# Moving the split operand tile to the end of on-chip memory in a one-core, two-block fp32 network

## The chip, the cores and the metric

The kernel runs on one core of a Trainium2 chip. That core has four engines which compute: TensorE (PE in the profile, with its weight loads as a row of their own, PEld), VectorE (DVE), ScalarE (ACT) and GpSimd (POOL). SyncE (SP) issues most of the DMAs. All of them run at the same time and meet at semaphores. The metric is the device time of one execution in microseconds, the median of several runs.

## What is computed

Input and output are one sequence of 256 tokens of width 1024 in float32. Two networks of two layers each follow one another.

```
def first_block(x, ...):                       # DEPTH = 2
    for i in range(DEPTH):
        if i % 2 == 0:
            mix = attention_mixer(x, ...)      # 8 windowed query heads over 2 key heads, 8 neighbourhood heads
        else:
            mix = mamba2_bidir_mixer(x, ...)   # 32 heads, both directions
        x = layer_norm(DN_ALPHA * x + mix, ...)
        x = layer_norm(DN_ALPHA * x + squared_relu_mlp(x, mlp_w1[i], mlp_w2[i]), ...)   # width 4096
...
def swiglu(h, w_gate, w_up, w_down):           # second block, twice in each of 2 layers, width 2816
    return (jax.nn.silu(h @ w_gate) * (h @ w_up)) @ w_down
```

The second block's layers are: half a swiglu, a mixer with a causal convolution on one half of the channels and differential attention on the other, and another swiglu, with an RMS norm ahead of each. Nearly all arithmetic is in products of the 256 tokens with weight matrices, all float32.

## The kernel before

**Work.** Weights come from HBM in units of 1 MB, that is 2048 floats in each of 128 partitions. A product is done at float32 accuracy with operands of the type float32r: weights and activations are each split into a high part (a cast) and a low part (the value less its high part), and three products are added in PSUM: high by high, low weight by high activation, high weight by low activation.

**The rings.** `w_raw`, `w_hi` and `w_lo` are rings of three units. SP loads a unit to `w_raw` (L626 and its like), ACT casts it to `w_hi` (L842), DVE (L1363), or POOL in some stages (L742), subtracts to `w_lo`, PE multiplies. Each step waits on semaphores for the one ahead, and for the slot of the ring to be free.

**The split operand.** `op` is the activations' counterpart: 16 chunks, each with a high half and a low half of 256 floats in every partition (`op_hi`, `op_lo`), 32 KB in each partition. ACT writes high halves (L857, L942 and some more), DVE low halves (L1401, L1509 and some more). No DMA touches it. PE reads it in two ways:

- as the moving operand, streamed past resident weights: `project_pair` (L2144 to L2148), where one matmul takes a whole chunk, high and low joined, as 512 columns against `w_hi`, and one takes the high half's 256 columns against `w_lo`; and `feature_chunk` (through L2070), where each of the three terms streams 256 columns of `op`;
- as the stationary operand, 128 columns loaded to the array, with 512 columns of `w_hi` or `w_lo` moving (`output`, `output_part` and `wide_tile`, through L2070).

**The loops.** `mlp` and `swiglu` are loops over groups of units: project one or two units to PSUM, let ACT and DVE form the hidden activations (into chunks 8 to 11 of `op`), multiply these by a unit of the second matrix into `acc`. The order of each engine's instructions is written out in the program, and nothing in it depends on where tiles lie.

**Placement.** Tiles are allocated one behind another in the order of the `sb(...)` lines. Each start is rounded up to a multiple of 32 bytes, and the first lies at byte 16,512 of the partition. Bytes within a partition:

| tile | before | after |
|---|---|---|
| `w_raw`, `w_hi`, `w_lo` | 16,512 to 90,240 | the same |
| `op` | 90,240 to 123,008 | 196,320 to 229,088 |
| `X` up to `g_pair`, 23 tiles | 123,008 to 165,600 | 90,240 to 132,832 |
| `arena` | 165,600 to 229,088 | 132,832 to 196,320 |

`arena` is carved by hand into each stage's own tiles. In the attention stage it starts with 2304 floats of constants, then `q_raw` 1024, `r_tmp` 1024, `k_raw` 256, `QT` 2048 and `KT`, six chunks of 256 floats. Heads 8 and 9 of the 16 read chunk 2 of `KT` at L2362, heads 12 and 13 chunk 4.

Of the kernel before, what the change touches and what calls it, by code (L numbers as in the profile page):

```python
# [9 lines left out]
F32R = mybir.dt.float32r  # L10
# [4 lines left out]
P = 128  # L15
T = 256
# [179 lines left out]
def two_blocks(nc, A, out):  # L196
    with ExitStack() as ctx:
        def sb(name, shape, dt=F32):
            return ctx.enter_context(nc.sbuf_tensor(name, shape, dt))
# [5 lines left out]
        w_raw = sb("w_raw", [P, RING, UN])  # L205
        w_hi = sb("w_hi", [P, RING, UN], F32R)
        w_lo = sb("w_lo", [P, RING, UN], F32R)
        op = sb("op", [P, 16, 2, T], F32R)
        op_hi, op_lo = op[:, :, 0, :], op[:, :, 1, :]
        X = sb("X", [P, TT, D])  # L210
        xn = sb("xn", [P, TT, D])
        turn_buf = sb("turn_buf", [P, 2, 2, T])
# [19 lines left out]
        g_pair = sb("g_pair", [P, TT, 2, P], F32R)  # L232
        AR = 15872
        arena = sb("arena", [P, AR])

        acc = ctx.enter_context(nc.psum_tensor("acc", [P, 4, 512], F32))
        pg = ctx.enter_context(nc.psum_tensor("pg", [P, 4, 512], F32))
# [2597 lines left out]
```

## Time and profile before

| | us |
|---|---|
| runs (3) | 1749.53, 1749.56, 1749.89 |
| median | 1749.56 |
| profiled execution: its span | 1748.3 |
| TensorE busy in that span | 1724.1 (99%) |
| VectorE busy | 1178.8 (67%) |
| ScalarE busy | 924.4 (53%) |
| GpSimd busy | 283.0 (16%) |

The page gives for the profiled execution its span alone, from the first to the last instruction; the median of the runs is 1.3 us above it. "Busy" of TensorE counts overlapping, pipelined matmuls, so 99% doesn't mean that its array is full: the distance between the starts of two matmuls says how fast it goes.

### The profile page before, as it was taken

The page shows a single profiled execution, that of the slowest core. Times are in us where ns is not written, and L with a number is a line of the kernel's source. Part 1 is how long each engine was busy: PE and PEld are TensorE (multiplying, and loading weights), DVE is VectorE, ACT ScalarE, POOL GpSimd, SP SyncE. Part 2 cuts the span into 40 slices and gives each one's busy share as a digit, 9 for nine tenths or more (in the row PEclk, how much of TensorE's full clock was granted, in tenths as well). Part 3 has the DMA queues.
Part 4 walks back from the last instruction along what each step waited for, and adds up shares of the span by engine and source line. Part 5 has one row for each costly group of instructions (what it writes and reads, how often), then busy time and mean ns, then how long its engine had stood idle before and what let it go on. Part 6 is the DMA issues. An engine that isn't in the chain of part 4 may idle for free.

```text
span 1748.3 us, 25220 instructions
## 1 busy us (share of the span) xinstructions
PE 1724.1 (99%) x9721; PEld 1472.5 (84%) x9721; DVE 1178.8 (67%) x1573; ACT 924.4 (53%) x1269; POOL 283.0 (16%) x154
## 2 busy tenths in 40 slices
PE   8999999999999999999999999999999999999999
PEld 7767888899798788878888978888888889878887
DVE  5767766778666776576666785666666667956665
ACT  4455444544675544455445666544554456665443
POOL 3000300376261040010000640000000006500000
PEclk9999999999999999999999999999999999999999
DMA  9314655564603575546555432655465555426652
GB/s 303 115 54 163 217 190 187 155 182 141 240 1 103 166 236 193 182 142 195 190 191 188 164 131 96 210 189 185 161 208 187 189 185 169 145 85 204 192 190 98
DMA packets 204268, 293.90 MB, mean 168 GB/s; under 512 B 6474, under 2 KB 169776, under 8 KB 204192
## 3 DMA queue, kind: packets, MB, share of 16 engines
q1 hardware_dynamic: 201072, 285.62, 50.3%
q0 software_dynamic: 2688, 6.47, 1.4%
q8 instruction: 52, 0.85, 0.2%
q10 hardware_dynamic: 432, 0.75, 0.1%
q14 instruction: 24, 0.20, 0.0%
HBM read 291.77 MB, written 1.05 MB: 167 GB/s over the span
## 4 chain that ended last, share of the span: by engine, by line
PE 92%; DVE 4%; ACT 3%; POOL 1%; issue 1%; DMA 0%; SPq 0%; ACTq 0%; DVEq 0%; POOLq 0%
PE acc L2070 30%; PE pg L2070 15%; PE pg L2144 12%; PE pg L2148 12%; PE pg L2147 6%; PE pg L2145 6%; PE acc L2575 1%; PE pg L2362 1%; PE pg L2562 1%; PE pg L2677 1%; PE pg L2190 1%; POOL w_lo L742 1%; ACT op L857 1%; DVE op L1401 1%; PE pg L2391 0%
## 5 line engine op out<-in xcount | busy, mean ns | idle before, releaser
L1363 DVE TENSOR_TENSOR w_lo<-w_raw,w_hi 128x2048 fp32r<-128x2048 f32 x231 | 538.9, 2334 | 162.9 <-ACT w_hi L842 162.8
L842 ACT CAST w_hi<-w_raw 128x2048 fp32r<-128x2048 f32 x269 | 513.0, 1908 | 70.8 <-PE pg L2070 28.3
L2070 PE MATMUL acc<-w_hi,op 128*128 128x512 f32 x1600 | 518.3, 393 | 1.7 <-DVE op L2000 1.6
L2144 PE MATMUL pg<-op,w_hi 128*128 128x512 f32 x960 | 382.3, 398 | 7.0 <-DVE op L1393 1.9
L2148 PE MATMUL pg<-op,w_hi 128*128 128x512 f32 x960 | 379.7, 396 | 0.0
L2070 PEld LDWEIGHTS acc<-w_hi,op 128*128 128x128 f32 x1600 | 300.4, 188 | 67.5 <-issue 8.6
L2070 PE MATMUL acc<-w_lo,op 128*128 128x512 f32 x800 | 311.5, 389 | 0.0
L742 POOL TENSOR_TENSOR w_lo<-w_raw,w_hi 128x2048 fp32r<-128x2048 f32 x38 | 175.1, 4615 | 682.6 <-DVE w_lo L1363 630.3
L2147 PE MATMUL pg<-op,w_lo 128*128 128x256 f32 x960 | 267.6, 279 | 0.0
L2145 PE MATMUL pg<-op,w_lo 128*128 128x256 f32 x960 | 266.3, 277 | 0.0
L2070 PE MATMUL pg<-op,w_hi 128*128 128x256 f32 x1184 | 222.6, 286 | 2.8 <-DVE op L1401 1.2
L2147 PEld LDWEIGHTS pg<-op,w_lo 128*128 128x128 f32 x960 | 180.2, 188 | 44.3 <-DVE op L1387 0.9
L2145 PEld LDWEIGHTS pg<-op,w_lo 128*128 128x128 f32 x960 | 180.5, 188 | 39.7
L2144 PEld LDWEIGHTS pg<-op,w_hi 128*128 128x128 f32 x960 | 182.1, 190 | 16.9 <-issue 4.8
L2070 PEld LDWEIGHTS pg<-op,w_hi 128*128 128x128 f32 x1184 | 187.3, 192 | 6.6 <-issue 3.1
L2148 PEld LDWEIGHTS pg<-op,w_hi 128*128 128x128 f32 x960 | 179.9, 187 | 0.0
L2070 PEld LDWEIGHTS acc<-w_lo,op 128*128 128x128 f32 x800 | 150.4, 188 | 30.0
L2070 PE MATMUL pg<-op,w_lo 128*128 128x256 f32 x592 | 167.6, 283 | 0.0
L942 ACT CAST op<-h 128x512 fp32r<-128x512 f32 x76 | 47.2, 621 | 215.1 <-PE acc L2070 189.8
L1509 DVE TENSOR_TENSOR op<-h,op 128x512 fp32r<-128x512 f32 x76 | 57.0, 750 | 84.9 <-ACT op L942 84.9
L2070 PEld LDWEIGHTS pg<-op,w_lo 128*128 128x128 f32 x592 | 113.7, 192 | 0.6 <-issue 0.5
L924 ACT COPY act_buf<-pg 128x512 f32<-128x512 f32 x44 | 25.8, 586 | 115.1 <-PE pg L2148 115.0
(348 smaller groups left out, 1735.5 us busy)
## 6 DMA issues: line engine op xcount, KB each, us to landing
w_raw<-in_mlp_w SPq DMA_DIRECT2D x64, 1024.0 KB, 5.3
w_raw<-in_ffn_w_gate SPq DMA_DIRECT2D x44, 1024.0 KB, 5.3
w_raw<-in_ffn_w_up SPq DMA_DIRECT2D x44, 1024.0 KB, 5.3
w_raw<-in_ffn_w_down SPq DMA_DIRECT2D x44, 1024.0 KB, 4.8
w_raw<-in_ssm_w_in SPq DMA_DIRECT2D x24, 1024.0 KB, 5.4
w_raw<-in_w_in SPq DMA_DIRECT2D x20, 1024.0 KB, 5.0
w_raw<-in_attn_w_in SPq DMA_DIRECT2D x8, 1024.0 KB, 10.6
w_raw<-in_ssm_w_out SPq DMA_DIRECT2D x8, 1024.0 KB, 4.9
```

Source lines behind the costliest of these rows:

```text
L742: pool.tensor_tensor(w_lo[:, r, :], w_raw[:, r, :], w_hi[:, r, :].bitcast(F32), ALU.subtract) \
L842: act.copy(w_hi[:, u % RING, :], w_raw[:, u % RING, :]).then_inc(hi_ready, 1)
L857: ins = act.activation(op_hi[:, j, :] if bias is None else turn_buf[:, b % 2, c, :], turn_out(name, b)[:, c * T:(c + 1) * T], ACT.Identity ...
L924: act.copy(act_pair, low_half(0)).then_inc(gate_lo, 1)
L942: act.copy(op_hi[:, at_chunk:at_chunk + 2, :], h32[:, :].rearrange("p (c t) -> p c t", c=2)).then_inc(h_hi, 1)
L1363: dve.tensor_tensor(w_lo[:, s, :], w_raw[:, s, :], w_hi[:, s, :].bitcast(F32), ALU.subtract) \
L1509: dve.tensor_tensor(op_lo[:, dst, :], h32[:, :].rearrange("p (c t) -> p c t", c=2), op_hi[:, dst, :].bitcast(F32), ALU.subtract).then_inc( ...
L2070: ins = pe.matmul(psum, l, r, start=first and i == 0, stop=last and i == 2)
L2144: pe.matmul(bank, hi, joined, start=k == 0, stop=False)
L2145: pe.matmul(bank[:, 0:T], lo, op_hi[:, k, :], start=False, stop=False)
L2147: pe.matmul(bank[:, 0:T], lo, op_hi[:, k, :], start=False, stop=False)
L2148: ins = pe.matmul(bank, hi, joined, start=False, stop=k == KC - 1)
```

## The change

The allocation of `op` moves from behind `w_lo` to behind `arena`. The tile's shape, its views and every instruction stay. Two kinds of addresses change: `op` starts 106,080 bytes further on, and everything that lay behind it (`X` to `arena`) starts 32,768 bytes earlier. The first step is an odd multiple of 32, the second a multiple of 128. The number and the order of the instructions on each engine are the same in both programs.

```
         w_lo = sb("w_lo", [P, RING, UN], F32R)
-        op = sb("op", [P, 16, 2, T], F32R)
-        op_hi, op_lo = op[:, :, 0, :], op[:, :, 1, :]
         X = sb("X", [P, TT, D])
...
         AR = 15872
         arena = sb("arena", [P, AR])
+        op = sb("op", [P, 16, 2, T], F32R)
+        op_hi, op_lo = op[:, :, 0, :], op[:, :, 1, :]
```

## Rows read from the trace of the kernel before

**Rows 1.** The page: span, busy time by engine, granted clock by slice
```profile
span 1748.3 us, 25220 instructions
...
PE 1724.1 (99%) x9721; PEld 1472.5 (84%) x9721; DVE 1178.8 (67%) x1573; ACT 924.4 (53%) x1269; POOL 283.0 (16%) x154
...
PEclk9999999999999999999999999999999999999999
```

**Rows 2.** The page: the chain that ended last, by engine
```profile
PE 92%; DVE 4%; ACT 3%; POOL 1%; issue 1%; DMA 0%; SPq 0%; ACTq 0%; DVEq 0%; POOLq 0%
```

**Rows 3.** The page: groups by line; out<-in (moving first), count | busy, mean ns | idle before
```profile
L2070 PE MATMUL acc<-w_hi,op 128*128 128x512 f32 x1600 | 518.3, 393 | 1.7 <-DVE op L2000 1.6
L2144 PE MATMUL pg<-op,w_hi 128*128 128x512 f32 x960 | 382.3, 398 | 7.0 <-DVE op L1393 1.9
L2148 PE MATMUL pg<-op,w_hi 128*128 128x512 f32 x960 | 379.7, 396 | 0.0
...
L2070 PE MATMUL acc<-w_lo,op 128*128 128x512 f32 x800 | 311.5, 389 | 0.0
...
L2147 PE MATMUL pg<-op,w_lo 128*128 128x256 f32 x960 | 267.6, 279 | 0.0
L2145 PE MATMUL pg<-op,w_lo 128*128 128x256 f32 x960 | 266.3, 277 | 0.0
L2070 PE MATMUL pg<-op,w_hi 128*128 128x256 f32 x1184 | 222.6, 286 | 2.8 <-DVE op L1401 1.2
...
L2070 PE MATMUL pg<-op,w_lo 128*128 128x256 f32 x592 | 167.6, 283 | 0.0
```

**Rows 4.** PE in order of time, swiglu loop, one cycle of four chunks: start, us
```profile
896.70 0.39 PE L2144 MATMUL pg<-op,w_hi 128*128 128x512 f32 x1
896.93 0.28 PE L2145 MATMUL pg<-op,w_lo 128*128 128x256 f32 x1
897.04 0.28 PE L2147 MATMUL pg<-op,w_lo 128*128 128x256 f32 x1
897.16 0.40 PE L2148 MATMUL pg<-op,w_hi 128*128 128x512 f32 x1
897.39 0.40 PE L2144 MATMUL pg<-op,w_hi 128*128 128x512 f32 x1
897.63 0.28 PE L2145 MATMUL pg<-op,w_lo 128*128 128x256 f32 x1
897.75 0.27 PE L2147 MATMUL pg<-op,w_lo 128*128 128x256 f32 x1
897.86 0.40 PE L2148 MATMUL pg<-op,w_hi 128*128 128x512 f32 x1
898.09 0.39 PE L2144 MATMUL pg<-op,w_hi 128*128 128x512 f32 x1
```

**Rows 5.** The same view just behind: `op` stationary, the rings moving
```profile
900.88 0.39 PE L2070 MATMUL acc<-w_hi,op 128*128 128x512 f32 x1
901.11 0.39 PE L2070 MATMUL acc<-w_lo,op 128*128 128x512 f32 x1
901.34 0.62 PE L2070 MATMUL acc<-w_hi,op 128*128 128x512 f32 x2
901.79 0.39 PE L2070 MATMUL acc<-w_lo,op 128*128 128x512 f32 x1
```

**Rows 6.** DVE in order of time in the same stretch, three successive slots
```profile
896.85 0.69 DVE L1496 TENSOR_TENSOR act_buf<-act_buf,xn 128x512 f32<-128x512 f32 x1
897.93 2.29 DVE L1363 TENSOR_TENSOR w_lo<-w_raw,w_hi 128x2048 fp32r<-128x2048 f32 x1 [0.39 <-ACT w_hi L842]
...
903.58 2.29 DVE L1363 TENSOR_TENSOR w_lo<-w_raw,w_hi 128x2048 fp32r<-128x2048 f32 x1 [0.33 <-ACT w_hi L842]
...
908.99 2.29 DVE L1363 TENSOR_TENSOR w_lo<-w_raw,w_hi 128x2048 fp32r<-128x2048 f32 x1 [1.12 <-ACT w_hi L842]
```

**Rows 7.** PE in order of time, state-space stage: operands from `g_pair` and `neg_tri`
```profile
475.76 0.34 PE L2562 MATMUL pg<-g_pair,select 128*128 128x384 f32 x1
475.94 0.28 PE L2564 MATMUL pg<-neg_tri,ident_r 128*128 128x256 f32 x1
476.05 0.34 PE L2562 MATMUL pg<-g_pair,select 128*128 128x384 f32 x1
```

**Rows 8.** PE in order of time: scores of heads 8, 9, 12 and 13
```profile
93.89 1.13 PE L2362 MATMUL pg<-arena 64*128 64x256 f32 x4
...
96.55 1.13 PE L2362 MATMUL pg<-arena 64*128 64x256 f32 x4
...
103.31 1.13 PE L2362 MATMUL pg<-arena 64*128 64x256 f32 x4
...
107.55 1.13 PE L2362 MATMUL pg<-arena 64*128 64x256 f32 x4
```

**Rows 9.** DVE by form, 512 floats; last, one line's min/median/max ns
```profile
L1509 DVE TENSOR_TENSOR op<-h,op 128x512 fp32r<-128x512 f32 x76 | 57.0, 750 | 84.9 <-ACT op L942 84.9
...
L1501 DVE TENSOR_TENSOR h<-pg,h 128x512 f32<-128x512 f32 x44 | 30.4, 691 | 55.5 <-ACT h L935 55.5
...
L1792 DVE TENSOR_TENSOR arena<-arena,acc 128x512 f32<-128x512 f32 x32 | 22.0, 687 | 24.0 <-POOL arena L789 23.7
...
L1393 DVE TENSOR_TENSOR op<-turn_buf,op 128x512 fp32r<-128x512 f32 x12 | 8.3, 692 | 0.4
...
L1509 DVE TENSOR_TENSOR op<-h,op x76: 687/692/2883, 156.9 to 1737.0; 128x512 fp32r<-128x512 f32 x76
```

**Rows 10.** ACT's groups by form, 512 floats in every partition
```profile
L942 ACT CAST op<-h 128x512 fp32r<-128x512 f32 x76 | 47.2, 621 | 215.1 <-PE acc L2070 189.8
...
L929 ACT ACTIVATE act_buf<-act_buf 128x512 f32<-128x512 f32 x44 | 27.7, 629 | 6.8 <-DVE act_buf L1496 6.8
...
L1007 ACT ACTIVATE arena<-arena 128x512 f32<-128x512 f32 x4 | 2.5, 632 | 1.1 <-DVE arena L1923 1.1
```

More of the change, by code:

```diff
@@ L207, in two_blocks @@
         w_lo = sb("w_lo", [P, RING, UN], F32R)
-        op = sb("op", [P, 16, 2, T], F32R)
-        op_hi, op_lo = op[:, :, 0, :], op[:, :, 1, :]
         X = sb("X", [P, TT, D])
@@ L234, in two_blocks @@
         arena = sb("arena", [P, AR])
+        op = sb("op", [P, 16, 2, T], F32R)
+        op_hi, op_lo = op[:, :, 0, :], op[:, :, 1, :]
         acc = ctx.enter_context(nc.psum_tensor("acc", [P, 4, 512], F32))
```

## The prediction

> **What bounds the kernel now.** I read the page from the top. The granted clock is full in every slice, so TensorE runs at its upper level, 2.4 GHz, throughout, and PE is busy for 1724.1 of 1748.3 us [rows 1]. The chain that ended last is PE for 92% of the span [rows 2]. The largest groups are all matmuls with `op` on one side and a weight ring on the other, and the idle time ahead of them is a few us in all [rows 3]. So the kernel is bound by the rate at which PE gets through its list, and it hardly ever waits for somebody. A change of addresses can move the end only if it changes how fast one matmul follows another, or if it makes writers of `op` so slow that PE has to wait for them.
>
> How fast is that rate? Rows of the time order give the distances between starts. Where 512 columns move, the next matmul starts 0.23 us later: three matmuls from 900.88 to 901.34 are 0.46 us for two, and five from 900.88 to 901.79 are 0.91 us for four, 227 to 228 ns each [rows 5]. At 2.4 GHz 512 columns are 213 ns, so about 14 ns lie between them. Where `op` moves, four chunks (four matmuls of 512 and four of 256 columns) take 898.09 - 896.70 = 1.39 us [rows 4]; 3072 columns are 1280 ns, so eight matmuls leave about 110 ns, again 14 ns each.
>
> **The change part by part.** It removes, adds and moves no instruction, no wait and no DMA. What it can alter is one of four things.
>
> (1) *The distance between `op` and the rings.* PE reads both at once. If neighbours in memory got in each other's way, the distance between starts would depend on which chunk meets which slot. In the trace it doesn't: L2144 to L2148 run through chunks 0 to 7, which start 24.6 to 38.9 kB behind the end of `w_hi`,, and rows 4 show the same 0.23 and 0.11 to 0.12 us steps from chunk to chunk; rows 5 take chunks 10 and 11 as stationary operand, with `w_hi` and `w_lo` moving in turn, and give 227 ns whichever ring moves. The 14 ns between matmuls are there when `op` moves, when it is stationary, and when neither tile is a ring or `op` [rows 7]: 384 columns are 160 ns, and the step is 475.94 - 475.76 = 0.18 us, the 256 columns behind it (107 ns) take 0.11. So they belong to each matmul, and not to the pair of addresses. Term: 0.
>
> (2) *Traffic of other engines next to `op`.* DVE writes `w_lo`, just ahead of `op`, from 897.93 to 900.22 [rows 6], and in rows 4 nothing happens at 897.93: the step from 897.86 to 898.09 is 0.23 us as before it. PE shows no sign of the others' traffic, and there is none for it to be freed from. Term: 0.
>
> (3) *The start of `op` no longer being a multiple of 64 bytes.* It goes from 90,240 (a multiple of 128) to 196,320, an odd multiple of 32. The trace has tiles that start so: `neg_tri`, `g_pair` and all of `arena`, whose starts before are odd multiples of 32. `g_pair` and `neg_tri` are float32r moving operands as `op` is, and their steps carry about the same 14 ns or less [rows 7]. For the writers: DVE's 512 floats take 692 ns into `op` (L1393) and 691 into `h32`, whose start is a multiple of 128 too, and 687 from and to `arena` [rows 9]; L1509's mean of 750 comes from a few long ones, up to 2883, its median being 692 as well [rows 9]. ACT's take 621 ns for the cast into `op`, 629 within `act_buf`, 632 within `arena` [rows 10]. Nothing tells an odd multiple of 32 from a rounder start by more than 5 ns, and of these writes some 76 of each kind are on hidden paths [rows 3, 9, 10]. Term: 0.
>
> (4) *The end of memory itself.* Here the trace gives a direct look, since `arena` covers these addresses before. Chunk 4 of `KT` starts 7680 floats into `arena`, at 165,600 + 30,720 = 196,320, the very byte at which `op` will start. Heads 12 and 13 stream it, heads 8 and 9 stream chunk 2, which lies below; all four take 1.13 us for their four matmuls [rows 8]. Term: 0.
>
> What no row shows is float32r at full rate with one tile at the far end. The nearest row that has any dependence on place is the cycle of rows 4: eight steps at (512 + 32)/2.4 and (256 + 32)/2.4, the spacing of rows 5 carried over, would be 4 x 227 + 4 x 120 = 1388 ns, and the cycle takes 1390 to 1395 as far as two decimals tell. That leaves at most 7 ns in a cycle that might hang on addresses. There are 960 L2144, two to a cycle, so 480 cycles and 3.4 us. I bound the unknown cost by it on both sides: -3.4 us if the new place loses this excess, +3.4 us if it doubles. The value that I take is 0, the row to which it is nearest being 7 and 8, where odd starts and the far end cost nothing.
>
> Sum on the profiled execution: 1748.3 + 0 = 1748.3 us; with the 1.3 us by which the runs' median stands above the span, 1749.6 us.
>
> There is one place where a rule and a row part. The rows give 227 ns from matmul to matmul with 512 columns [rows 5]. The Trainium skill, on the page TensorE: Matmul & The Clock Gate, section Back-to-back issue gap, gives N/2.4 + 2.5, that is 216 ns, for an isolated stream; an estimate by that page would call 11 ns of each step avoidable, and somebody might lay them to memory. The same page says that the moving operand and the weight load have read ports of their own, by which the place of `op` doesn't matter, and the page SBUF — State Buffer, section Who interferes with whom, says that PE never waits on another engine for memory. On that the trace agrees, with rows 4 and 6.
>
> **The rivals.**
>
> *Slower: an odd start costs each stream from `op` a little.* The mechanism would be at the head of each moving read. The place is L2144 to L2148 and L2070's 256-column form: 1920 reads of 512 columns and 1920 + 1184 + 592 = 3696 of 256 [rows 3], together 5616, and all of them are on the path. One clock period of 0.42 ns each is 2.3 us, three are 7.0 us (1756.6), and 6 ns, the largest difference between steps of one kind that rows 4 could hide, would be 34 us (1783). It decides from 0.62 ns per read, which is 3.5 us. For it: these 5616 reads are back to back and have no slack. Against it: rows 7 and 8, where operands start oddly and the steps are no longer. What makes me keep it is that rows 7 are short bursts.
>
> *Faster: `op` and the rings do disturb each other now.* If the 14 ns between matmuls, or a part of them, came from two reads that meet in one stretch of memory, the move would give it back. One tenth of it, 1.4 ns on the 5616 and on the 2400 with `op` stationary [rows 3], is 11 us (1738); the small form is the 3.4 us of the cycle's excess (1746.2). Against it: the steps are the same for chunks at any distance and for tiles that aren't `op` or rings [rows 4, 5, 7].
>
> *Writers become late.* ACT's and DVE's writes to `op` could be longer by some ns. L942 ends a chain that PE meets only in the next group: ACT waits 215.1 us in sum for PE's side ahead of it [rows 10], so PE is ahead in need by microseconds, and 10 ns on each of 76 + 76 writes is 1.5 us hidden. Only at the turns between stages does PE wait on DVE's writes; its idle time ahead of L2144 is 7.0 us in sum [rows 3], and 2% more on it would be 0.1 us. This is inside "same".
>
> *The change doesn't do what it says.* The tile could be placed where it was. By the allocation order it isn't, but then too the time is 1749.6.
>
> **How the numbers follow.** 0.2% of 1749.6 is 3.5 us, about what a measurement of this kernel can tell from no change. No effect, or one under that: 0.78. The odd start costs something that can be seen: 0.13. The move frees something that can be seen: 0.09. The likeliest case gives 1749.6. The range takes in the bounds of the unknown cost, 1746.2 and 1753.0, and on the slower side three periods per read, 1756.6, because of its greater chance.
>
> **What would show it.** In the changed kernel's profile the steps of a cycle of four chunks should again sum to 1.39 us, those of the 512-column matmuls with `op` stationary to 0.23 each, the head scores to 1.13, DVE's 512 floats into `op` to 0.69 and ACT's to 0.62. If the slower rival holds, the steps of L2144 to L2148 grow and those of L2070's acc form stay, since there `op` doesn't move. If the faster one holds, both shrink below 227 and 120. The prediction is wrong if a float32r stream or weight load from the far end, at full rate, isn't what bursts there are, or if DVE's writes and PE's reads meet at the new place as they don't at the old.

## The result

The changed kernel takes 1774.72 us (median of 4 runs, 1774.46 to 1774.95) against 1749.6 us before: a ratio of 1.0143, with a 95% interval of 1.0131 to 1.0155. Moving one tile, with no instruction changed, costs 25 us. The forecast was no change.

The page of the changed kernel first: span, busy times and TensorE's groups (moving operand named first, count | busy us, mean ns | idle before).

```profile
span 1773.1 us, 25220 instructions
...
PE 1749.4 (99%) x9721; PEld 1480.1 (83%) x9721; DVE 1178.9 (66%) x1573; ACT 924.6 (52%) x1269; POOL 282.7 (16%) x154
...
L2070 PE MATMUL acc<-w_hi,op 128*128 128x512 f32 x1600 | 528.3, 399 | 1.7 <-DVE op L2000 1.6
L2144 PE MATMUL pg<-op,w_hi 128*128 128x512 f32 x960 | 380.8, 397 | 6.9 <-DVE op L1393 1.9
L2148 PE MATMUL pg<-op,w_hi 128*128 128x512 f32 x960 | 379.5, 395 | 0.0
...
L2070 PE MATMUL acc<-w_lo,op 128*128 128x512 f32 x800 | 316.9, 396 | 0.0
...
L2147 PE MATMUL pg<-op,w_lo 128*128 128x256 f32 x960 | 272.6, 284 | 0.0
L2145 PE MATMUL pg<-op,w_lo 128*128 128x256 f32 x960 | 269.0, 280 | 0.0
L2070 PE MATMUL pg<-op,w_hi 128*128 128x256 f32 x1184 | 222.5, 286 | 2.8 <-DVE op L1401 1.1
```

DVE and ACT are as busy as before, to 0.2 us [rows 1], and PE's idle time ahead of its groups is the same [rows 3]. So nobody waits more; PE itself is slower. The means of the matmul groups say where, against [rows 3]: with `op` stationary (L2070 to `acc`) 393 ns becomes 399 and 389 becomes 396; L2147 goes from 279 to 284, L2145 from 277 to 280; L2144, L2148 and the 256-column form of L2070 stay within 1 ns.

The distances between starts are surer than these modelled durations. PE in order of time, changed kernel, one swiglu group: its 24 matmuls with `op` stationary start at 912.77, and the next projection at 918.39.

```profile
912.77 0.39 PE L2070 MATMUL acc<-w_hi,op 128*128 128x512 f32 x1
913.00 0.40 PE L2070 MATMUL acc<-w_lo,op 128*128 128x512 f32 x1
913.24 0.63 PE L2070 MATMUL acc<-w_hi,op 128*128 128x512 f32 x2
...
918.39 0.39 PE L2144 MATMUL pg<-op,w_hi 128*128 128x512 f32 x1
918.62 0.28 PE L2145 MATMUL pg<-op,w_lo 128*128 128x256 f32 x1
...
919.80 0.39 PE L2144 MATMUL pg<-op,w_hi 128*128 128x512 f32 x1
```

In the kernel before, the same block starts at 900.88 [rows 5] and ends with this row:

```profile
906.32 0.39 PE L2144 MATMUL pg<-op,w_hi 128*128 128x512 f32 x1
```

That is 5.62 us for 24 steps, 234 ns each, against 5.44 us, 227 ns each. The cycle of four chunks takes 919.80 - 918.39 = 1.41 us against 1.39 [rows 4]. A swiglu group has one such block and eight cycles: 0.18 + 8 x 0.02 = 0.34 us. ACT in order of time, line L942, which runs once in a group, shows the same: the changed kernel first,

```profile
901.67 0.62 ACT L942 CAST op<-h 128x512 fp32r<-128x512 f32 x1 [3.14 <-PE acc L2070]
918.59 0.62 ACT L942 CAST op<-h 128x512 fp32r<-128x512 f32 x1 [3.14 <-PE acc L2070]
```

then the kernel before.

```profile
889.94 0.62 ACT L942 CAST op<-h 128x512 fp32r<-128x512 f32 x1 [2.97 <-PE acc L2070]
906.52 0.62 ACT L942 CAST op<-h 128x512 fp32r<-128x512 f32 x1 [2.97 <-PE acc L2070]
```

A group lasts 16.92 us, and lasted 16.58. The whole falls out of such steps. Summed over all distances between starts in the two traces, the matmuls with `op` stationary account for +17 us, those of `project_pair` for +9 and the three-term form with `op` moving for 0; together 26, of which some 1 us is won back elsewhere.

### The profile page after: what moved, and what is told of

It reads as the page before. It is cut to its first block, busy times and chain, and to the rows that moved or that the text cites. A ratio compares the mean times of both kernels' runs of the same rounds, so it can differ in the third digit from the quotient of the medians.

```text
span 1773.1 us, 25220 instructions
## 1 busy us (share of the span) xinstructions
PE 1749.4 (99%) x9721; PEld 1480.1 (83%) x9721; DVE 1178.9 (66%) x1573; ACT 924.6 (52%) x1269; POOL 282.7 (16%) x154
## 4 chain that ended last, share of the span: by engine, by line
PE 92%; DVE 3%; ACT 3%; POOL 1%; issue 1%; DMA 0%; SPq 0%; ACTq 0%; DVEq 0%; POOLq 0%
PE acc L2070 31%; PE pg L2070 15%; PE pg L2144 12%; PE pg L2148 12%; PE pg L2147 6%; PE pg L2145 6%; PE acc L2575 1%; PE pg L2362 1%; PE pg L2562 1%; PE pg L2677 1%; PE pg L2190 1%; POOL w_lo L742 1%; ACT op L857 1%; DVE op L1401 1%; PE acc L2391 0%
## 5 line engine op out<-in xcount | busy, mean ns | idle before, releaser
L2070 PE MATMUL acc<-w_hi,op 128*128 128x512 f32 x1600 | 528.3, 399 | 1.7 <-DVE op L2000 1.6
L2144 PE MATMUL pg<-op,w_hi 128*128 128x512 f32 x960 | 380.8, 397 | 6.9 <-DVE op L1393 1.9
L2148 PE MATMUL pg<-op,w_hi 128*128 128x512 f32 x960 | 379.5, 395 | 0.0
L2070 PEld LDWEIGHTS acc<-w_hi,op 128*128 128x128 f32 x1600 | 301.1, 188 | 76.1 <-issue 8.5
L2070 PE MATMUL acc<-w_lo,op 128*128 128x512 f32 x800 | 316.9, 396 | 0.0
L2147 PE MATMUL pg<-op,w_lo 128*128 128x256 f32 x960 | 272.6, 284 | 0.0
L2145 PE MATMUL pg<-op,w_lo 128*128 128x256 f32 x960 | 269.0, 280 | 0.0
L2070 PE MATMUL pg<-op,w_hi 128*128 128x256 f32 x1184 | 222.5, 286 | 2.8 <-DVE op L1401 1.1
L2145 PEld LDWEIGHTS pg<-op,w_lo 128*128 128x128 f32 x960 | 180.2, 188 | 43.5
L2147 PEld LDWEIGHTS pg<-op,w_lo 128*128 128x128 f32 x960 | 180.2, 188 | 43.2 <-DVE op L1387 0.9
L2144 PEld LDWEIGHTS pg<-op,w_hi 128*128 128x128 f32 x960 | 180.1, 188 | 17.2 <-issue 4.8
L2070 PEld LDWEIGHTS pg<-op,w_hi 128*128 128x128 f32 x1184 | 184.6, 188 | 6.8 <-issue 3.1
L2148 PEld LDWEIGHTS pg<-op,w_hi 128*128 128x128 f32 x960 | 181.8, 189 | 0.0
L2070 PEld LDWEIGHTS acc<-w_lo,op 128*128 128x128 f32 x800 | 150.9, 189 | 34.3
L2070 PE MATMUL pg<-op,w_lo 128*128 128x256 f32 x592 | 166.4, 281 | 0.0
L942 ACT CAST op<-h 128x512 fp32r<-128x512 f32 x76 | 47.2, 620 | 226.4 <-PE acc L2070 201.1
L2070 PEld LDWEIGHTS pg<-op,w_lo 128*128 128x128 f32 x592 | 112.0, 189 | 0.6 <-issue 0.5
```

What stands on the lines that cost most here:

```text
L942: act.copy(op_hi[:, at_chunk:at_chunk + 2, :], h32[:, :].rearrange("p (c t) -> p c t", c=2)).then_inc(h_hi, 1)
L2070: ins = pe.matmul(psum, l, r, start=first and i == 0, stop=last and i == 2)
L2144: pe.matmul(bank, hi, joined, start=k == 0, stop=False)
L2145: pe.matmul(bank[:, 0:T], lo, op_hi[:, k, :], start=False, stop=False)
L2147: pe.matmul(bank[:, 0:T], lo, op_hi[:, k, :], start=False, stop=False)
L2148: ins = pe.matmul(bank, hi, joined, start=False, stop=k == KC - 1)
```

## The experiments

Unless said otherwise each kernel is the kernel before or the changed one with a pad, and computes the whole network. "Offset" is how far `op`'s start lies behind that of the kernel before, taken within 256 bytes; the changed kernel's is 106,080 = 414 x 256 + 96, so 96. Single runs were taken next to a run of the kernel before on the same chip, which gave 1749.84, 1749.61 and 1750.30 us.

### Is it the odd start, or the end of memory?

Theory A: an odd multiple of 32 bytes as start costs the reads. Theory B: the far end of memory, or the distance to the rings. (e2 has a second pad of 8 floats behind `op`, so that all tiles behind it move by 64 bytes.)

```
 (changed kernel)                               # e1_end_64; e5_end_in_phase: [P, 40]
         arena = sb("arena", [P, AR])
+        pad0 = sb("pad0", [P, 8])
         op = sb("op", [P, 16, 2, T], F32R)
...
 (kernel before)                                # e2_near_32; e3: 16, e6: 24, e7: 32 floats
         w_lo = sb("w_lo", [P, RING, UN], F32R)
+        pad0 = sb("pad0", [P, 8])
         op = sb("op", [P, 16, 2, T], F32R)
...
 (changed kernel, op taken from the end)        # e4_mid_64
         g_pair = sb("g_pair", [P, TT, 2, P], F32R)
+        pad0 = sb("pad0", [P, 8])
+        op = sb("op", [P, 16, 2, T], F32R)
         arena = sb("arena", [P, AR])
```

At the end, 32 bytes later, a multiple of 128:

> op stays at the end but starts 32 bytes later, at 196,352, a multiple of 128. Theory A (the odd multiple of 32 as start costs PE): back to the time before, 1749.6 us within 1 us, and 227 ns from start to start where op is stationary. Theory B (the far end of memory, or the distance to the rings, costs PE): as the changed kernel, 1774.7 us within 1 us, 234 ns.

Measured 1763.37 us: neither. Behind the rings, 32 bytes later:

> op behind the rings as before but 32 bytes later, at 90,272, an odd multiple of 32; what lies behind it moves by 64 bytes. Theory A: 1774.7 us within 2 us. Theory B: 1749.6 us within 1 us.

Measured 1757.71 us: neither. Behind the rings, 64 bytes later:

> op behind the rings but 64 bytes later, at 90,304, an odd multiple of 64; what lies behind it moves by 64 bytes. Theory A with a grid of 64 bytes: 1749.6 us within 1 us. If the grid is 128 bytes, or if the offset of op against the rings within some larger power of two counts: slower, up to 1775 us. Theory B: 1749.6 us.

Measured 1757.70 us. In the middle of memory:

> op between g_pair and arena, at 132,864, a multiple of 128; arena behind it starts at a multiple of 64. Theory A: 1749.6 us within 1 us. Theory B: between 1749.6 and 1774.7 us, since the tile is at 43 kB behind the rings' end instead of 106 kB.

Measured 1763.46 us. Both theories fall: a start at a multiple of 128 doesn't give the old time (e1, e4), and the tile next to the rings doesn't either (e2, e3). But the middle and the end, 63 kB apart, agree to 0.1 us, and their starts have one thing in common: both are multiples of 256, offset 128. That made theory C, that only the offset within 256 bytes counts, and four runs to break it.

> op at the end, but at 196,480, which leaves the same remainder by 256 (128) as 90,240 and as the rings' starts. Theory C (op's start against the rings' starts, counted within 256 bytes, sets the steps): 1749.8 us within 1 us and 227 ns with op stationary. Theory B (the far end or the distance): above 1760 us, as the two other places away from the rings. If C's period is longer than 256 bytes: anything between.

Measured 1749.64 us.

> op behind the rings, 96 bytes later than before (90,336), the remainder that the changed kernel has within 256. Theory C: 1774.7 us within 1.5 us. Theory B, or a period above 256 bytes: another time, under B 1749.8 to 1758 us.

Measured 1775.03 us.

> op behind the rings, 128 bytes later than before (90,368), a multiple of 256. Theory C: 1763.4 us within 1.5 us, as the two kernels with op at a multiple of 256 at the end and in the middle. Theory B: 1749.8 to 1758 us.

Measured 1763.21 us. All three are as C has it: at the end of memory with offset 0 the kernel is as fast as before, and next to the rings with the changed kernel's offset it is as slow as the changed kernel. The last one moves all tiles together, by a pad ahead of `w_raw`:

```
+        pad0 = sb("pad0", [P, 8])
         w_raw = sb("w_raw", [P, RING, UN])
```

> Rings, op and all other tiles 32 bytes later, so op and rings stand to each other as before and each starts at an odd multiple of 32. Theory C in its relative form (only the difference counts): 1749.8 us within 1 us. Theory D (the place of a start within a line of memory counts by itself): 1757.7 us or more, as with op alone 32 bytes later.

Measured 1749.61 us. Here the rings and `op` all start at odd multiples of 32, and it costs nothing; what counts is the difference between them, as far as this one shift of 32 bytes tells. The pages of e8 (first) and e5 (second) show the groups of the kernel before to the nanosecond [rows 3]:

```profile
span 1747.8 us, 25220 instructions
...
L2071 PE MATMUL acc<-w_hi,op 128*128 128x512 f32 x1600 | 518.3, 393 | 1.7 <-DVE op L2001 1.6
...
L2071 PE MATMUL acc<-w_lo,op 128*128 128x512 f32 x800 | 311.5, 389 | 0.0
...
L2148 PE MATMUL pg<-op,w_lo 128*128 128x256 f32 x960 | 267.6, 279 | 0.0
```

```profile
span 1747.8 us, 25220 instructions
...
L2145 PE MATMUL pg<-op,w_hi 128*128 128x512 f32 x960 | 382.3, 398 | 7.0 <-DVE op L1394 1.9
...
L2146 PE MATMUL pg<-op,w_lo 128*128 128x256 f32 x960 | 266.3, 277 | 0.0
```

### The other offsets

The same pad with 40, 48 and 56 floats, and 16 bytes by a view into a wider tile:

```
-        op = sb("op", [P, 16, 2, T], F32R)
+        op_room = sb("op_room", [P, 16 * 2 * T + 8], F32R)
+        op = op_room[:, 4:4 + 16 * 2 * T].rearrange("p (c x t) -> p c x t", c=16, x=2)
```

> op 160 bytes later, that is 96 bytes short of the next 256. Theory C1 (the same cost for the same distance on either side of a multiple of 256): 1775 us. Theory C2 (the order of the two reads counts, so the sides differ): another time than 1775 by over 2 us.

Measured 1767.47 us.

> op 192 bytes later, 64 short of the next 256. C1: 1757.7 us. C2: another time by over 2 us.

Measured 1747.18 us.

> op 224 bytes later, 32 short of the next 256. C1: 1757.7 us. C2: another time by over 2 us; if the cost rises with the difference up to 256, near 1775 us or more, and if there is a better place than 0, below 1749 us.

Measured 1766.85 us.

> op 16 bytes later, in its own room. If the cost goes by steps of 32 bytes: 1749.6 us (with the lower step) or 1757.7 us (with the upper). If it goes by bytes: near 1753.7 us.

Measured 1754.87 us. The sides differ (C2): there is no symmetry about 0 and no steady rise, 16 bytes already count, and at 192 the network is faster than before.

### Whose reads meet?

The order of the offsets has no simple form, so the next question was who is involved. A kernel without the network: two float32r tiles, filled once, and then TensorE alone.

```
            for i in range(16):  # 512 columns, offset 4 bytes
                pe.matmul(acc[:, i % 2, 0:512], st[:, i % 8 * P:i % 8 * P + P], mv[:, 1:513], start=True, stop=True)
```

> No network: two float32r tiles whose starts have the same remainder by 256, and nothing but TensorE at work. Groups of 16 matmuls, weights always from multiples of 512 bytes in the one, the moving operand from offset 0, 4, 8, ... 252 bytes in the other, first with 512 and then with 256 columns; the output is the input. Theory E (TensorE's own two reads, the moving operand and the next weights, meet in memory): the step of a group depends on the offset, as in the network, by some ns (227 ns at 0, 234 at some others). Theory F (writes or reads of the other engines meet TensorE's reads): the same step at every offset, within 1 ns.

PE in order of time, one row for 16 matmuls (the last number), each at its own offset: 0, 4, 8 and 12 bytes, then 192, 196 and 200.

```profile
24.24 3.79 PE L53 MATMUL acc<-mv,st 128*128 128x512 f32 x16
27.87 3.94 PE L55 MATMUL acc<-mv,st 128*128 128x512 f32 x16
31.65 3.89 PE L57 MATMUL acc<-mv,st 128*128 128x512 f32 x16
35.38 3.82 PE L59 MATMUL acc<-mv,st 128*128 128x512 f32 x16
...
202.86 3.90 PE L149 MATMUL acc<-mv,st 128*128 128x512 f32 x16
206.59 4.00 PE L151 MATMUL acc<-mv,st 128*128 128x512 f32 x16
210.43 3.89 PE L153 MATMUL acc<-mv,st 128*128 128x512 f32 x16
```

From start to start: (27.87 - 24.24)/16 = 227 ns at offset 0, 236 at 4, 233 at 8, and (210.43 - 206.59)/16 = 240 at 196. With 256 columns the steps run from 113 to 123 ns. The page of this kernel says that hardly anybody else worked; DVE's 2.2 us are the copies that fill the tiles and take the result:

```profile
PE 378.0 (97%) x2113; PEld 328.9 (84%) x2113; DVE 2.2 (1%) x5; POOL 0.2 (0%) x4
```

Theory E holds here, and F falls: the dependence needs TensorE alone, and its range, 227 to 240 ns, covers the 227 to 234 ns that the network's blocks with `op` stationary took at the offsets tried. This probe moves one operand only; that the difference counts, and not that operand's own start, rests on e8. The second probe put pairs of offsets (against `w_hi` and against `w_lo`) through the network's three sequences, and a third did so at the network's own addresses.

> No network, TensorE alone: the kernel's three sequences of matmuls (chunks in joined form, three terms with op moving, three terms with op stationary) for every pair of offsets of op against w_hi and against w_lo, 0 to 224 bytes in steps of 32. Theory E: where both offsets are equal, the mean steps order the offsets as the network's times do (192 shortest, then 0, then 32 and 64; 96 longest); with unequal offsets some pair is shorter than all of these. Theory F: no dependence.

It spans 227.8 to 234.5 ns with `op` stationary and 113.6 to 122.5 ns in the three-term form with `op` moving. Both offsets at 0 are among the best, both at 96 the worst of the equal ones, as in the network; but 192 came out 14 us slow, where the network is fast. So the order was met in part only.

> No network, TensorE alone, the output is the input: the network's three sequences (joined chunks moving, three terms with op moving, three terms with op stationary) at the network's own addresses, for all 256 pairs of offsets of op against w_hi and w_lo in steps of 16 bytes. Theory E, that TensorE's own two reads explain the whole effect: mean steps weighted with the network's counts give, where both offsets are equal, +25 us for 96 bytes, +14 for 128, +18 for 160, +17 for 224, +8 for 32 and 64, +5 for 16 and -3 for 192, each within 3 us. If the other engines have a share, they differ from the network's by more.

Mean steps, worked out from the starts in the probe's trace (without the first and last four steps of each pair sequence and the first and last three of the others) and multiplied with the network's counts (3840 matmuls of the pair form, 1872 with `op` moving, 2640 with `op` stationary), beside the network:

| offset, bytes | TensorE alone, us against offset 0 | network, us against the kernel before in the same job |
|---|---|---|
| 16 | -12.8 | +4.6 |
| 32 | +8.2 | +7.9 |
| 64 | +9.1 | +7.9 |
| 96 | +21.8 | +25.4 |
| 128 | +14.1 | +13.6 |
| 144 | -16.0 | +11.1 |
| 160 | +21.4 | +17.2 |
| 192 | +9.9 | -3.1 |
| 224 | +20.4 | +16.6 |

With all steps counted, the middle column changes by up to 2.4 us. Six of the nine agree within 4.2 us, without another engine at work; only three of them (32, 64, 128) within the 3 us that were expected. Three more (16, 144, 192) are off by 13 to 27 us. So TensorE alone shows the effect and most of its size at 96 bytes (21.8 of 25.4 us), but by this run's own terms a share of the other engines isn't ruled out. The last three runs tested what can be built on the table.

### A better place?

```
+        op_room = sb("op_room", [P, 16 * 2 * T + 40], F32R)      # e16: starts 144 bytes later
+        op = op_room[:, 36:36 + 16 * 2 * T].rearrange("p (c x t) -> p c x t", c=16, x=2)
...
+        pad0 = sb("pad0", [P, 32])                               # e17
         w_lo = sb("w_lo", [P, RING, UN], F32R)
+        pad1 = sb("pad1", [P, 16])
         op = sb("op", [P, 16, 2, T], F32R)
```

> op 144 bytes later than before, the place for which TensorE alone had the shortest weighted steps (-16 us). Theory E with the probe's table taken as it stands: 1733.6 us. If the steps in the network also hang on what came before (the offset of 16 bytes had -13 us in the probe and +5 in the network): anywhere from 1734 to 1760 us.

Measured 1760.74 us, a ratio of 1.0064 (1.0047 to 1.0080): the table's best place is slower than before. In the probe at this offset the blocks with `op` stationary ran at 226.7 ns; in the network the mean of the same step was 233 ns. At 16 bytes too the probe settled at 226.7 ns, after a step or two. The network at 16 bytes (e12) did both: of its 71 blocks of 24 such matmuls, 31 took 227 ns per step on average and 33 took 233. Two blocks that follow one another in a swiglu loop, from e12's trace in order of time, each with the matmuls just ahead of it, the start of the projection behind it, and ACT's first work in it:

```profile
853.53 0.28 PE L2146 MATMUL pg<-op_room,w_lo 128*128 128x256 f32 x1
853.64 0.28 PE L2148 MATMUL pg<-op_room,w_lo 128*128 128x256 f32 x1
853.76 0.40 PE L2149 MATMUL pg<-op_room,w_hi 128*128 128x512 f32 x1
854.00 0.40 PE L2071 MATMUL acc<-w_hi,op_room 128*128 128x512 f32 x1
...
859.45 0.39 PE L2145 MATMUL pg<-op_room,w_hi 128*128 128x512 f32 x1
...
854.27 0.59 ACT L936 COPY h<-pg 128x512 f32<-128x512 f32 x1 [2.72 <-PE pg L2149]
```

```profile
870.13 0.28 PE L2146 MATMUL pg<-op_room,w_lo 128*128 128x256 f32 x1
870.26 0.28 PE L2148 MATMUL pg<-op_room,w_lo 128*128 128x256 f32 x1
870.37 0.40 PE L2149 MATMUL pg<-op_room,w_hi 128*128 128x512 f32 x1
870.60 0.39 PE L2071 MATMUL acc<-w_hi,op_room 128*128 128x512 f32 x1
...
876.20 0.39 PE L2145 MATMUL pg<-op_room,w_hi 128*128 128x512 f32 x1
...
870.88 0.59 ACT L936 COPY h<-pg 128x512 f32<-128x512 f32 x1 [2.73 <-PE pg L2149]
```

The first block takes 5.45 us, 227 ns per step, the second 5.60 us, 233. Both read the same slot of the rings and the same chunks of `op`; ACT starts 0.27 and 0.28 us behind the block's start, and DVE (L1502) 0.89 us behind it in both. What differs is TensorE's own steps ahead of the block: the starts from L2146 to L2149 are 0.11 and 0.12 us apart in the first, 0.13 and 0.11 in the second. So at 16 bytes the stream has two rhythms at the same addresses, and the steps just before go with which of them it takes. That the same holds at 144 and 192 bytes is not shown.

> op 192 bytes against w_hi and 64 bytes against w_lo. By the probe's table 6 us below the kernel before: 1743.5 us. If only op against w_hi counted: 1747.2 us, as with both at 192. If only op against w_lo counted: 1757.7 us, as with both at 64.

Measured 1746.24 us, ratio 0.9981 (0.9971 to 0.9990): between the table's 1743.5 and the 1747.2 of `w_hi` alone.

> The same place as the fastest so far, op 192 bytes later, timed in rounds: 1747.2 us within 0.5 us, 0.1 to 0.2% below the kernel before.

Measured 1746.62 us (1744.68 to 1748.26 over 10 runs), ratio 0.9983 (0.9973 to 0.9993), 0.1 us outside what was expected. This is e10's kernel again. Both beat the kernel before by 0.2%. e17 rules out that `w_lo` alone counts, since 64 there would give 1757.7. The times don't rule out that `w_hi` alone does: the runs of the two overlap. The groups do tell them apart. The page of e18, then that of e17:

```profile
L2145 PE MATMUL pg<-op,w_hi 128*128 128x512 f32 x960 | 385.1, 401 | 7.0 <-DVE op L1394 1.9
...
L2148 PE MATMUL pg<-op,w_lo 128*128 128x256 f32 x960 | 266.0, 277 | 0.0
```

```profile
L2146 PE MATMUL pg<-op,w_hi 128*128 128x512 f32 x960 | 379.7, 396 | 7.0 <-DVE op L1395 1.9
...
L2149 PE MATMUL pg<-op,w_lo 128*128 128x256 f32 x960 | 270.1, 281 | 0.0
```

With the same offset against `w_hi`, the first matmul of a chunk pair goes from 401 to 396 ns and the `w_lo` one from 277 to 281: the other ring's offset counts as well, and here its effects nearly cancel. e18's ten runs also spread over 3.6 us, where e17's spread over 0.8. In e10, the same program, the 256-column steps of L2071 with `op` moving against `w_lo` were 116 ns on average against 115 in e18.

## Why the prediction was wrong

**What bounds the kernel** was read rightly: PE's rate from matmul to matmul does, and a change of addresses had two ways to matter, of which the first, "how fast one matmul follows another", is the one that came true.

**Part (1), the distance between `op` and the rings, is the step that failed.** It said that the trace tries many distances, and that the step is the same at all of them. It does try many, but all of one kind: a chunk of `op` is 2048 bytes, its halves 1024, a token half 512, a slot of a ring 8192, a weight slice 512. Every one is a multiple of 256, so all matmuls between `op` and the rings stood at offset 0. Rows 5 are of chunks 8 and 9, not 10 and 11 as it says, which changes nothing for the same reason. Nor was rows 7's pair of other tiles at another offset: `neg_tri` and `ident_r` start at 162,016 and 163,040, 1024 bytes apart, and `select` is one column repeated. The argument took "many distances" for "all distances", and never asked what they had in common. The term was put at 0 and measured 25 us: the runs showed 5 us at 16 bytes, 25 us at 96 at either end of memory (the changed kernel and e6), and nothing at 106,240, which is 415 x 256 (e5). The 14 ns between matmuls are there at offset 0, and what the move adds comes on top, 7 ns with `op` stationary.

**Part (2)** is not contradicted: TensorE alone shows the effect, and of the 25.4 us at 96 bytes it gives 21.8. Whether the other engines have a part in the rest, and in the three offsets that the last probe missed, was not tested.

**Part (3), the odd start,** has the right term for the wrong question. An odd multiple of 32 costs nothing by itself (e8), and DVE's and ACT's writes into `op` kept their 750 and 620 ns. But the change turned two things at once, the start's own remainder and the difference to the rings, and only the first was priced. Rows 7, taken as evidence on float32r, are bursts of two matmuls; the text said so and gave it too little weight. Rows 8 are plain float32 with other shapes, and `QT` and `KT` lie a multiple of 1024 bytes apart, so at one offset again.

**Part (4)** was right: the end of memory costs nothing (e5).

**The bound of 3.4 us** was the term that was mis-sized. The cycle of rows 4 did carry a sign of the effect: worked out to the ns, its steps with 512 columns are 230, 233, 236 and 233, for one and the same form, against 227 in rows 5. Its excess over rows 5's spacing was taken as the bound for what addresses can do; it is only what they do at one offset. The first probe's span, 227 to 240 ns, gives as an estimate up to 13 ns on each of some 4,500 matmuls with 512 columns, 60 us, as a bound on the slow side.

**The rivals.** The slower one had the right sign, and its forms from 7 to 34 us take in the 25, but that is luck, since the mechanism was another: it would have left the `acc` form of L2070 as it was, and that form grew most. The faster one, "`op` and the rings do disturb each other now", had the right parties, and the range's 3.4 us below was met by the place at 192 bytes (-3.1 us), but it expected the distance to free PE. That the two reads depend on each other's place was in it; that a move would as likely hit a worse offset as a better one was not. The time of 1774.7 us lies above the range's 1756.6.

**The rules of the skill.** The Trainium skill (TensorE: Matmul & The Clock Gate, section Step-by-step: what each phase is for) says that loading the next weights takes no read bandwidth from the running matmul. The Trainium skill (SBUF — State Buffer, section Who interferes with whom) says that PE never waits on anyone. No run here shows the second to be wrong, and the two blocks of e12 at 227 and 233 ns, with ACT and DVE at the same places, agree with it. The first doesn't fit so well: with float32r and TensorE alone, the step goes from 227 to 240 ns with the offset of the two operands (e13), and there the measurement decides, though no run shows that it is the two reads that meet.

**What stays open.** That the moving stream and a weight load meet in memory is a reading that fits a dependence on the difference of two addresses, the same again after multiples of 256 bytes, on TensorE alone; it is argued, not shown. Whether it is the weights of the same matmul or of the next, and why an offset is good or bad, was not told apart, and neither was why the probe and the network differ at 144 and 192 bytes.

## What to carry to other kernels

Where TensorE is the bound and float32r tiles feed it from both sides, the start of the one against the start of the other, within 256 bytes, is a parameter of the kernel, worth -0.2% to +1.4% here; a tile that is added, resized or moved ahead of either can change the time of code that nobody touched, so compare steps from start to start before blaming the edit. The cheap fix is to keep the old remainder with a pad (e5). To choose a new one, time the whole kernel: the probe of TensorE alone was right on six offsets of nine, and its best pick was slower than the start.

## What the runs showed of the hardware that was not expected

- float32r matmuls at the granted clock of 1.0 (2.4 GHz) follow each other at 226.7 ns for 512 columns and 119 ns for 256 at offset 0, and at up to 240 ns for 512 and 113 to 123 ns for 256 at others, with no other engine at work (e13).
- Moving both operands together by 32 bytes changed nothing (1749.61 against 1749.61 us); moving one by 16 bytes cost 5 us.
- Equal offsets at places 42 to 106 kB apart gave equal times to 0.3 us: 1763.2, 1763.4 and 1763.5 at 128 bytes, 1774.7 and 1775.0 at 96, 1749.6 and 1749.6 at 0.
- At 144 bytes the same sequence ran at 226.7 ns in the probe (e15) and at 233 in the network (e16). At 16 bytes blocks at the same addresses in one execution of the network ran at 227 or at 233 ns (e12).
